# New tables of places for the expert slots of a decoder step on one core, without the matmuls of zeros

## What is computed

```python
q = (xt @ w_q).reshape(PEER_BLOCK, PEER_HEADS, 2, PEER_HALF)
s1 = jnp.einsum('thk,nk->thn', q[:, :, 0], sub_keys[0]).astype(jnp.float32)
s2 = jnp.einsum('thk,nk->thn', q[:, :, 1], sub_keys[1]).astype(jnp.float32)
...
idx = e1 * N_KEYS + e2
g = jax.nn.softmax(top, axis=-1).astype(xt.dtype)
act = jax.nn.gelu(jnp.einsum('thkd,td->thk', u_tab[idx], xt))
return jnp.einsum('thk,thkd->td', g * act, v_tab[idx])
```

## Time and profile before

| | |
|---|---|
| runs | 2004.1, 2020.93, 2021.28 us; median 2020.93 |
| profiled execution | span 2136.8 us, the only time recorded of it |
| instructions | 25746 |
| TensorE's mean granted clock | 0.814 of full speed |

### The profile page before, as it was taken

One profiled execution on the slowest core, in us unless ns is written; L12 is line 12 of the kernel. 1 busy time (PEld: TensorE's weight loads), 2 busy tenths in 40 slices (PEclk: granted clock), 3 DMA queues, 4 the chain that ended last, 5 costly groups with the idle time before them and its releaser, 6 DMA issues.

```text
span 2136.8 us, 25746 instructions
## 1 busy us (share of the span) xinstructions
PE 1549.0 (72%) x9280; PEld 752.4 (35%) x9280; DVE 1321.9 (62%) x3189; ACT 353.4 (17%) x934; POOL 1185.7 (55%) x1097
## 2 busy tenths in 40 slices
PE   5863767867579799878785999897877741563765
PEld 2453233522135346524442456534423310111211
DVE  2369886887776555488676756587885336434442
ACT  0210121111122111112131211131312110010011
POOL 0023665566776645467646645577675257744655
PEclk8887878987687897988887897997988785777777
DMA  9868989999999999999969799999998989999998
GB/s 371 314 236 346 365 330 347 391 396 382 347 346 348 359 404 373 361 414 347 382 212 345 271 375 401 378 345 349 367 337 303 352 309 343 402 417 370 377 349 306
DMA packets 213941, 751.57 MB, mean 352 GB/s; under 512 B 27236, under 2 KB 35628, under 8 KB 213816
## 3 DMA queue, kind: packets, MB, share of 16 engines
q0 software_dynamic: 155136, 564.20, 69.8%
q1 hardware_dynamic: 58680, 185.72, 22.4%
HBM read 747.74 MB, written 2.10 MB: 351 GB/s over the span
## 4 chain that ended last, share of the span: by engine, by line
PE 43%; DVE 14%; DMA 13%; issue 12%; POOL 8%; another core or an unknown queue 7%; ACT 2%; SPq 1%; DVEq 0%; POOLq 0%; ACTq 0%
PE yacc L1274 13%; DMA vring<-in_peer_v,expert 6%; POOL uring L813 4%; PE pp L1062 4%; DVE uring L2046 4%; POOL vring L813 3%; PE pp L1036 3%; PE pp L1125 3%; PE pq L1125 2%; PE ps L1160 2%; PE ps L870 2%; PE pp L1197 1%; DMA uring<-in_peer_u,expert 1%; PE ps L1184 1%
## 5 line engine op out<-in xcount | busy, mean ns | idle before, releaser
L813 POOL DMA_INDIRECT uring<-in_peer_u,expert x512 | 571.5, 1116 | 471.1 <-DVE dots L2046 191.1
L1274 PE MATMUL yacc<-vring,diag 64*64 64x512 f32 x4096 | 659.3, 727 | 230.1 <-DMA vring<-in_peer_v,expert 118.0
L813 POOL DMA_INDIRECT vring<-in_peer_v,expert x512 | 542.2, 1059 | 430.6 <-PE yacc L1274 263.3
L2046 DVE CUSTOM_DVE_ANT_0 uring<-uring,h 128x1024 f32<-128x1024 f32 x512 | 614.9, 1226 | 201.2 <-DMA uring<-in_peer_u,expert 175.7
L1274 PEld LDWEIGHTS yacc<-vring,diag 64*64 64x64 f32 x4096 | 158.0, 154 | 589.1 <-issue 345.5
L1566 ACT ACTIVATE diag<-cst,wts 128x64 f32<-128x64 f32 (+1 forms) x528 | 155.4, 338 | 470.4 <-PE yacc L1274 229.9
L1062 PE MATMUL pp<-hT,wring 128*128 128x128 f32 x1024 | 128.9, 287 | 10.4 <-DMA wring<-in_peer_w_q 4.6
L1062 PEld LDWEIGHTS pp<-hT,wring 128*128 128x128 f32 x1024 | 124.1, 202 | 28.1 <-issue 26.2
L1929 DVE TENSOR_REDUCE arena<-arena 128x16 f32<-128x1024 f32 x64 | 77.8, 1216 | 63.8 <-ACT arena L1505 58.8
L1317 ACT ACTIVATE arena<-ps 128x512 f32<-128x512 f32 (+6 forms) x77 | 39.9, 532 | 253.4 <-remote 76.9
L1125 PE MATMUL pp<-w_uk,arena 128*128 128x512 f32 x128 | 75.3, 677 | 3.4 <-issue 2.7
(11 more groups left out here) (306 smaller groups left out, 1823.0 us busy)
## 6 DMA issues: line engine op xcount, KB each, us to landing
wring<-in_peer_w_q SPq DMA_DIRECT2D x48, 1024.0 KB
wring<-in_sg_w_in SPq DMA_DIRECT2D x48, 768.0 KB
wring<-in_w_mod SPq DMA_DIRECT2D x35, 1024.0 KB
wring<-in_sg_w_out SPq DMA_DIRECT2D x18, 1024.0 KB
uring<-in_w_mod SPq DMA_DIRECT2D x9, 1024.0 KB, 12.7
wring<-in_mla_w_o SPq DMA_DIRECT2D x9, 1024.0 KB
uring<-in_peer_u,expert POOLq DMA_INDIRECT x512
vring<-in_peer_v,expert POOLq DMA_INDIRECT x512
```

The source lines that it names most:

```text
L813: pool.indirect_dma_start(ring[:, slot % RING, :], None, table[n // 3], bass.IndirectOffsetOnAxis(ap=idx, axis=0)).then_inc(land[slot % RI ...
L1274: last = pe.matmul(yacc[64 * q:64 * q + 64, r], diag[at, slot % RING, :], v[at, 512 * q:512 * q + 512], start=first, stop=final)
L2046: dve.tensor_tensor_reduce(u, u, rows_h[:, :], 1.0, 0.0, ALU.mult, ALU.add, dots[:, p % 2, i:i + 1]).then_inc(u_used, 1)
```

## The change

All five tables are new. In the new ones a slot stands only where a list scheduler found no stage instruction ready on the engine; the letters come in longer runs. The 48 N are gone from `PLAN_PE` (of these 41 sent a matmul; the profile holds their 82 records). `load_mod_bias` waits for `cleared` itself, since ten chunks now are loaded ahead of the place where SP waited for it. The list of stages, all operations of a slot, the rings and their sizes are as before.

```diff
 PLAN_PE = """
-52:N 75:N 120:N 148:N 152:N 157:V 158:V 159:V 160:V 169:VV 170:VV 171:V 173:V 174:V 176:V 180:V 184:V 189:VV 192:VVV
...
+181:VVVVVVVVVVVVVVVV 186:VV 190:VVVVVV 191:V 195:VVVVVVV 199:VV 201:VVVV 203:V 206:VVVVV 209:VV 211:VV 228:VVVV 229:VV
...
+1119:VVVVVVVVVVVVVVVVVVVVVVVVVVVVVVVVVVVVVVVVVVVVVVVVVVVVVVVVVVVVVVVVVVV 1122:V 1123:VVVVVV
 """
 PLAN_ACT = """
-111:T 116:DDDDD 121:D 123:D 131:DDD 132:D 136:DDD 138:D 143:D 146:T 147:DDD 148:D 149:DD 150:DD 154:DDD 158:DD 159:DD
...
+127:TDDDDDDDDDDDDDDDD 141:T 144:DDDDDDDDD 146:DDDDDD 147:D 152:T 153:DDDDDDDD 154:DDD 156:DD 158:DDD 162:TDDDDD 163:DD
...
 PLAN_DVE = """
-190:U 206:U 208:U 213:U 220:U 240:U 241:UU 256:U 259:UU 274:U 289:U 293:UU 294:U 303:P 304:U 313:U 329:W 333:U 342:U
...
+209:U 210:U 225:U 230:U 259:U 264:U 276:UUU 304:U 313:U 317:U 321:U 325:U 330:U 333:U 335:PUW 344:U 346:UU 347:U 351:U
...
 PLAN_POOL = """
-UUUVUUUUUUUUVUUUVVUVUUUVUUVUUVUUUUVUUVVUVVVVUVVUVUUVVUUUUUUUVVVUVVUUUVUUVUVUVVUUUUUVUVUVUVUUUUVVUVUVUUUUUUUUUUUVVUUUU
...
+UUUUUUVUUUUVUVVUVUVVUUUUUUUUUUUUVUVVVVVVVUVUUVUVUVUVVUVUUUUUUUUUUUUVVUUUVVVVVVVVUVUUUUUVVUVVVUUVVUUUVVUVVUUVUVVUVUVUUUV
...
 PLAN_SP = """
-0:WWW 1:WW 2:WWW 7:WWWWW 31:WWW 32:W 33:WWWWWW 37:WW 52:W 53:W 56:WWW 57:W 59:WW 64:W 66:W 72:WW 75:W 76:W 80:W
...
+0:WWWWWWWWWW 31:W 32:WWWWWW 33:WW 111:WWWWWWWWWWWWWWWWWWWWWWWWWWWWWWWWW 162:W 166:WWWWWW 168:WWWWWWWWWW 170:W 172:W
...
@@ -710,6 +686,8 @@
             def load_mod_bias(row):
 
                 _, l, j = MODS[MOD_ROW * row]
+                if row == 0:
+                    sp.wait_ge(cleared, 5)
                 before = [r for r in range(row) if (r in KR_ROWS) == (row in KR_ROWS)]
```

More of the change, by code:

```diff
@@ new lines @@
+336:V 337:VV 349:VVV 352:VVV 354:VVVVVVVVVV 372:V 373:V 374:VV 376:VV 387:V 389:V 390:VVVVVVV 391:V 399:V 411:VVVVVV
+418:V 420:VV 443:VV 453:V 456:VV 482:V 484:V 497:VVVV 503:VV 522:VVV 524:V 527:V 528:V 532:V 547:V 549:V 555:V
+560:VVVV 563:VV 564:VV 568:VVV 571:VV 572:VV 576:VVVV 589:VVVVVVVVV 590:VVV 591:VV 597:V 599:V 600:V 602:V 622:V
+629:VVVV 633:V 636:V 640:V 643:V 646:V 647:VVVVVVVV 648:V 649:VVV 659:VVVVV 668:VVVVVVVVVVVVVV 669:V 684:VVVVVVVVVVV
+685:VV 686:VV 694:V 708:VV 731:VVV 736:V 738:VV 757:V 759:V 771:V 777:VV 778:V 784:V 799:V 802:V 806:VVV 807:VV 831:VV
@@ L132 @@
+844:VVVVVVV 845:VVVVVVVVVVVVVV 846:V 847:VV 856:V 859:V 862:VVVVVVVV 863:VV 864:VVV 870:V 872:V 894:VV 900:VVVVV
+911:VV 918:VV 920:VVVVVVVVV 921:V 922:VV 938:VVV 941:VVVVVVVVVVVVVVVV 942:VV 957:VVVVVVVVVVVVVV 959:VV 967:VV 971:V
+997:VVVVV 1002:V 1004:V 1010:VVVVVV 1016:VVVVVVVVVVV 1042:VV 1043:V 1054:VVV 1055:V 1057:V 1064:VVV 1067:V 1072:V
+1075:VVV 1083:VVV 1088:VVV 1104:VVVVV 1105:VV 1113:V
+1119:VVVVVVVVVVVVVVVVVVVVVVVVVVVVVVVVVVVVVVVVVVVVVVVVVVVVVVVVVVVVVVVVVVV 1122:V 1123:VVVVVV
 """
 PLAN_ACT = """
[L134 removed]
@@ new lines @@
+408:DD 414:T 415:DDDDDDD 417:DD 423:DD 428:T 430:DDDDDDDDDDDD 431:DD 434:DDD 444:D 448:D 449:DD 457:T 459:DDD 461:DD
+466:DD 468:D 469:D 470:DDDDDTDDD 471:DD 476:DDDDD 480:DDDDD 484:DDD 494:Y 500:T 502:DDDDDD 505:DDDDDDDDDD 525:TD
+532:DDDDDDDDDDD 549:DDT 552:DD 555:DD 556:DDD 558:D 568:D 570:DD 571:DDDD 579:DTD 584:DD 585:DD 588:DDDD 593:DDDDDD
+596:DD 597:D 600:TDDDDDDD 610:D 612:D 615:DDDDDDDTDDDDD 616:D 633:DDDDD 634:DDDD 646:D 650:T 653:DDD 655:DDDDDDDDD
+656:DDD 661:D 669:TDDDDDDDDDDDDDDDD 690:TYDDDDDDDDDDDDDDDD 715:T 716:DDDDDDD 717:D 718:DDD 719:DDD 721:D 727:D
@@ new lines @@
+854:UUUUUU 863:UUU 864:P 866:WU 867:UU 869:UUUUU 891:UUUUUU 904:UU 915:PUWU 916:U 917:UU 919:U 928:UUU 938:UU 946:U
+948:U 952:UUUPW 955:U 958:UU 966:UU 971:U 974:U 1009:UUUUUUUU 1038:UPWUUU 1040:UUU 1060:UUU 1061:UUUU 1065:U 1074:U
+1097:UUUPUUWUUUU 1142:UU 1167:U 1168:U 1173:UU 1193:UUUP 1195:UWUUUU 1196:UUUUU 1197:U 1199:U 1200:UU 1201:U 1204:PWU
+1210:U 1211:U 1217:U 1223:UU 1237:UU 1277:UU 1296:UU 1299:UU 1304:U 1307:UUPW 1309:UUUUU 1313:UU 1316:UUUUU 1320:U
+1330:UU 1331:PUW 1334:U 1337:UU 1347:UUU 1439:UUUUUUU 1443:UUP 1448:WU 1450:UU 1451:UU 1465:U 1469:U 1471:U 1473:U
@@ new lines @@
+1479:UUU 1494:U 1495:U 1517:UUUU 1518:PWUUUUUUUUU 1554:UUUUU 1555:UPUW 1558:U 1559:UU 1562:U 1570:UUUUU 1572:U 1574:U
+1599:UUUPUUW 1600:U 1627:UUU 1637:U 1658:UU 1661:U 1669:U 1688:UU 1693:U 1696:UUPUUWUUU 1699:U 1703:UUUU 1713:U 1718:U
+1719:U 1720:U 1724:U 1725:UP 1726:UW 1737:U 1774:UUU 1777:U 1806:UUU 1808:UUUU 1810:U 1812:UU 1814:PUW 1815:U 1818:UUU
+1819:U 1828:U 1836:UU 1838:U 1848:U 1913:UUU 1914:UUU 1915:P 1919:UWU 1920:U 1938:UUU 1940:UU 1941:UU 1942:U 1945:UU
+1948:UUP 1950:UW 1961:U 1962:UUUU 1986:UU 1988:UUUU 2016:U 2018:UUU 2019:PW 2049:UUU 2053:UUUUUPUWUUUUUUU 2105:UUU
@@ L198 @@
+173:W 177:W 211:WWWWWWW 316:W 327:WWWWWWWW 328:WWWWWWWWWWWWWWWWWWWWWWWWW 352:WWWWW 354:WWWWWWW 440:W
+441:WWWWWWWWWWWWWWWWWWWWWWWWWWWWW 502:WWWWWWWWWWWWWWWW 510:W 514:WWW 515:WWWWWW
 """
```

93 lines of the change are left out of this document (22 added, 71 removed).

## The result

The changed kernel takes 2063.45 us (median of four runs, 2055.33 to 2077.45), the kernel before 2019.83: the ratio is 1.024 with an interval of 1.018 to 1.030. It is slower by 44 us, where 26 us of gain were forecast.

A forecast was written before the change was run, and what follows sets the result against it. DMA-bound where fed (419 GB/s), with 343 us of the profiled 2136.8 lost where it isn't. Terms 10 + 10 + 4 + 3 = 27 us, 25.5 on the median, gave 1995 us (chance 0.45), range 1935 to 2075.

The forecast's parts named there:

- the sign that I named: Sign of a wrong forecast: in the changed profile, more than two holes with a DMA share under 0.5 behind 1000 us.
- The first sums: At the start, four w_mod chunks ahead of TensorE's first sum fill a DMA hole: 10 us won, bounds 0 and 12.2.
- The cache stages: TensorE's long stretches of cache keys without a sum, with gathers U ordered to cover them: 10 us won, bounds -14 and 31.
- The last step: At the end, POOL's wait for the sample's list goes because VectorE makes it earlier: 4 us won, between 0 and 14.2.
- The zeros: Leaving out 41 matmuls of zeros frees 20 us of TensorE, mostly hidden by waits for gathers: 3 us won.
- SP: Ten chunks loaded ahead of tile A's rows; norm A at worst 1 or 2 us late: booked at nothing.
- The tail of gathers alone: Last step: more gathers run with no weights beside them; up to 15 us might be lost, nothing booked.
- Weights right behind gelu: On VectorE, 23 instead of 197 dots between gelu and weights, so it waits through ScalarE's tanh: nothing booked.
- The lockstep rival: Each of 33 steps hands a ScalarE wait to VectorE and POOL, 71 us less 27: 2062 us, chance 0.12.
- the keys' rival: Five instead of one stretches of cache keys without a sum make full DMA holes: 71 us slower, 2088 us, chance 0.16.
- No change: Gather-only stretches keep 357 GB/s whatever the order, holes move but stay, under 20 us won: 2010 to 2030 us, chance 0.22.
- The clock rival: Half the zeros each kept a 7 us TensorE stretch fast; losing them costs 33 us less 27: within 1%, chance 0.05.

The follow-up runs named there:

- h_start: Kernel before, without zeros and with SP's old table, but with the new places for slots 0 to 23: 2037.19 us, ratio 1.010.
- b_again: The kernel before, unchanged, run and profiled again: 2015.55 us, ratio 1.001; its profile spans 2014.4 us.
- b_nozero: The kernel before with the 48 letters N (zeros) left out, nothing else: 2010.37 us, ratio 0.9965.
- b_runs_dve: Kernel before without zeros, each dot on VectorE moved on to the next place where the new table has one: 2139.41 us, ratio 1.060.
- a_zeros: The changed kernel with the 48 letters N (zeros) put back at their old places: 2062.91 us, ratio 1.023 against the kernel before.
- a_w_late: Changed kernel with the weights W moved back behind up to as many dots as in the old tables: 2132.8 us, ratio 1.057 against the kernel before.

## Why the prediction was wrong

**What failed.** Two steps. The first is the reading of the bound: I booked gains by the holes in one profiled execution, 5.7% above the median, and 10 of the 27 us by holes that a second profile does not have. The second turned the sign: the prediction let the gather-only stretches keep their rate whatever the order, and booked nothing for the new order on VectorE. There the changed kernel loses its time: 206 us of DMA time with gathers alone, where it was 146, and some 60 us more behind POOL's waits for a dot. It is a loss spread thin. Behind 1000 us the changed profile has one hole of 10 us at under half the rate (the list, at 1667 us), so the sign that I named, more than two such holes, stayed away though the kernel is slower.

Term by term:

- *The first sums*, forecast 10: right at its place. 8.2 us from 200 to 220 us, 8.8 us at 75 MB in h_start; in the changed kernel 13.8 against b_again and 11.4 against b_nozero. No run shows that it reaches the end: h_start loses it at its seam.
- *The cache stages*, forecast 10, bounds -14 and 31: this term had nothing under it. The 31 us of holes belonged to that one execution; the fresh profile has 389 and 394 GB/s there. The stretches of keys that pass without a sum do not cost either: the DMA time lost in POOL's waits of 1 us and more for a place of V is 16 us before and 8 after. POOL's wait for TensorE did come out below 265.7 us, as the sign for this term said, at 226.3, but that was no sign: the fresh profile of the kernel before has 196.3.
- *The last step*, forecast 4: the wait at the end is gone, as said, but the list of layer 0 is waited for 19.3 us in one piece. Lost before: 17 x (1 - 272/419) = 6.0 and 10 x (1 - 155/419) = 6.3 us; after: 19 x (1 - 145/419) = 12.4. Net nothing. The tail of gathers alone, on which I nearly booked 15 us, runs at 413 GB/s.
- *The zeros*, forecast 3: 7 us in the old order, 0 in the new, at a clock 0.003 lower without them in the one and some 0.01 lower in the other.
- *SP*, booked at nothing: right.
- *Weights right behind gelu*, booked at nothing "as U runs 15 slots ahead and VectorE is 62% busy": the cover I named was wrong for the old order, where the move costs 43 us. In the new one, whose table for ScalarE has the tanh ready, some 7 us are left of it by my estimate.

**The missing term: how dots stand on VectorE.** The new table has dots at 209 places of VectorE where the old one had 334. I counted the output columns of TensorE between sums and never the dots in a row on VectorE. Measured in the changed kernel's trace, runs of three and more lose 29 us more DMA time than before, of the 48 in all. Shown are the slow gathers during such a run, that the DMA loses nothing by them in the window with three weight chunks beside, and that more such runs (b_runs_dve) lose more. Shown is also that the new order's loss stands behind POOL's waits for dots and not behind those for sums. Not shown is the share of the 44 us that would come back without the runs: every edit that would have told it moved entries against each other too.

**The rivals.** The lockstep rival's 2062 us meets the measured 2063 by luck: its sign (VectorE idle ahead of the weights) shows 21 us in the changed kernel, not 71. Of the keys' rival neither the holes nor the waits came. "No change" was wrong by the interval. The clock rival's stretches of 7 us stood on no row; a_zeros, with the zeros back and no time gained, speaks against it. The 358 GB/s of a core's HBM share, which the Trainium skill gives ("DMA: Bandwidth & Descriptors", "Where 436 GB/s comes from"), did not bind this kernel, which runs on one core: the trace disagrees once more, with 373 GB/s over a whole execution.

**What stays open.** 23 us of the added lost time lie outside of dots. Part may be the aftermath of the runs. Rows of V wait longer for their weights in a ring of seven (1638 us in sum, 450 before), which is a strong rival; but the loss behind waits for a sum, which a_w_late raises to 114 us, is 30 us in the changed kernel and 37 to 43 in the old order, so it is not there that this shows. How the loss behind the dots divides between slow gathers and fewer gathers in flight when the wait ends is not told apart. Whether the order on VectorE alone, with the others fitted to it, would bring the 44 us back was not tried.

**The best version** is the old one without its zeros, b_nozero: 0.35% faster than the kernel before, 2.6% faster than the changed one.

## What to carry to other kernels

Before you cost a change by a hole in a profile, hold that execution's span against the median of the runs; if they differ by more than the gain you look for, take a second profile. When gathers are issued by an engine that another one slows, look at that other one's longest run of the disturbing operation, not at its busy share, and see what else feeds the queue meanwhile. A sum of waits does not price them: ask instead, for each piece of DMA time that is lost, what the issuing engine had last waited for. Orders made as a whole must be tested as a whole: here every edit of the slots on one engine alone, in either direction, was slower than the kernel it started from.

## What the runs showed of the hardware that was not expected

- A gather that POOL issues while VectorE computes a dot (128x1024, 1.23 us) takes up to 2.0 us instead of 0.94; in the middle of a run of dots two starts are 2.29 us apart, against 1.24 us without. With one engine to issue them that is 229 against 422 GB/s.
- It is not dots alone. Beside a SCALAR_TENSOR_TENSOR of 128x1536 a gather takes up to 2.10 us (two rows of the changed kernel below). But the gathers that overlap only a TENSOR_REDUCE of 128x1024 (39 in the changed kernel, 40 before) all take 0.93 to 0.95 us. So it depends on the operation of VectorE, and not on VectorE being busy.

```profile
790.36 1.76 DVE L1957 SCALAR_TENSOR_TENSOR arena<-arena 128x1536 f32<-128x1536 f32 x1 [8.37 <-ACT arena L1295]
790.84 2.10 POOL L791 DMA_INDIRECT vring<-in_peer_v,expert  x1 [8.04 <-PE yacc L1252]
```

- With gathers alone the rate goes with what is in flight, counted here as the bytes issued and not yet moved, in gathers of 0.524 MB: in stretches of 10 us of the fresh profile 314 to 337 GB/s between one and two (by how the stretches are cut), 379 to 391 between two and three, 419 above three.
- 41 matmuls of zeros cost 7 us in one order and nothing in another. Without them the granted clock was 0.003 lower in the one (profiled executions) and some 0.01 lower in the other (0.802 to 0.810 against 0.810 to 0.821), and no time hung on it.
